# mLSTM's small f32 products in pairs of half arrays, and the prompt's negative maxima from one VectorE reduction

## The reference, cut to what matters

```python
qk = jnp.einsum('bthd,bshd->btsh', qc, kc) * w
num = jnp.einsum('btsh,bshe->bthe', qk, vc) + sc[..., None] * jnp.einsum('bhed,bthd->bthe', C, qc)
...
C_new = sl[..., None, None] * C + jnp.einsum('bsh,bshe,bshd->bhed', wl, vc, kc)
n_new = sl[..., None] * n + jnp.einsum('bsh,bshd->bhd', wl, kc)
```

## Time and profile before

| what | us |
|---|---|
| median of three runs (lowest, highest) | 1054.78 (1048.41, 1056.2) |
| the profiled execution: its time | 1056.03 |
| its span, first to last instruction | 1054.3 |
| TensorE busy | 1004.5 (95%) |
| VectorE busy | 615.4 (58%) |
| ScalarE busy, GpSimd busy | 403.9 (38%), 151.6 (14%) |
| mean granted TensorE clock, as a share of full speed | 0.985 |
| the mLSTM heads and what leads into the samples' attention | 285 to 372 |
| the prompt's attention, from the first maximum to the last value product | about 459 to 552 |

### The profile page before, as it was taken

One profiled execution on the slowest core, in us unless ns is written; L12 is line 12 of the kernel. 1 busy time (PEld: TensorE's weight loads), 2 busy tenths in 40 slices (PEclk: granted clock), 3 DMA queues, 4 the chain that ended last, 5 costly groups with the idle time before them and its releaser, 6 DMA issues.

```text
span 1054.3 us, 19143 instructions
## 1 busy us (share of the span) xinstructions
PE 1004.5 (95%) x7704; PEld 906.4 (86%) x7704; DVE 615.4 (58%) x1314; ACT 403.9 (38%) x759; POOL 151.6 (14%) x206
## 2 busy tenths in 40 slices
PE   4999999999999979989889999999999999999996
PEld 4999999899866647665559999999999999999996
DVE  3736753444358666677967556575757577832222
ACT  5223422333143455438764333333333334622222
POOL 3200020330112211016740000000000000000000
PEclk9999999999989999989999999999999999999998
DMA  6561162653611165344012222222222222423222
GB/s 188 194 179 41 44 200 72 244 185 145 244 37 52 53 255 210 117 121 136 1 55 103 82 82 84 83 83 82 82 82 82 82 82 57 119 68 87 77 55 90
DMA packets 82109, 114.29 MB, mean 108 GB/s; under 512 B 10075, under 2 KB 72681, under 8 KB 79296
## 3 DMA queue, kind: packets, MB, share of 16 engines
q1 hardware_dynamic: 75280, 70.60, 21.8%
q0 software_dynamic: 6768, 42.84, 11.0%
HBM read 103.33 MB, written 13.59 MB: 111 GB/s over the span
## 4 chain that ended last, share of the span: by engine, by line
PE 85%; DVE 8%; ACT 2%; issue 2%; DMA 1%; POOL 1%; SPq 0%; DVEq 0%; ACTq 0%
PE banks L1627 14%; PE banks L1625 12%; PE banks L1665 6%; PE banks L1128 6%; PE banks L1075 5%; PE banks L1664 5%; PE banks L1078 4%; PE banks L1079 4%; PE banks L1582 3%; PE banks L1112 3%; PE banks L1581 2%; PE banks L1696 2%; PE banks L1403 1%; PE banks L1339 1%; PE banks L1328 1%
## 5 line engine op out<-in xcount | busy, mean ns | idle before, releaser
L1627 PE MATMUL banks<-xnT_r,RB_r 128*128 128x320 f32 x352 | 109.6, 311 | 0.0
L1627 PE MATMUL banks<-xnT_r,ring_r 128*128 128x320 f32 x352 | 109.3, 311 | 0.0
L1625 PE MATMUL banks<-xnT_r,RB_r 128*128 128x256 f32 x352 | 103.1, 293 | 0.0
L1625 PE MATMUL banks<-xnT_r,ring_r 128*128 128x256 f32 x352 | 98.8, 281 | 0.0
L1627 PE MATMUL banks<-RC_r,RB_r 128*128 128x320 f32 x264 | 82.3, 312 | 0.0
L1625 PE MATMUL banks<-RC_r,RB_r 128*128 128x256 f32 x264 | 74.2, 281 | 0.0
L1128 PE MATMUL banks<-RA,RB 128*128 128x128 f32 (+1 forms) x512 | 71.0, 280 | 2.5 <-ACT RA L667 2.5
L2363 DVE TENSOR_TENSOR ring_r<-ring,RB_r 128x2048 fp32r<-128x2048 f32 x22 | 49.4, 2288 | 37.4 <-ACT RB_r L887 37.4
L1625 PEld LDWEIGHTS banks<-xnT_r,RB_r 128*128 128x128 f32 x352 | 67.0, 190 | 1.8
L1128 PEld LDWEIGHTS banks<-RA,RB 128*128 128x128 f32 x512 | 64.1, 188 | 4.0 <-ACT RA L667 3.9
L1625 PEld LDWEIGHTS banks<-xnT_r,ring_r 128*128 128x128 f32 x352 | 67.4, 192 | 0.0
(11 more groups left out here) (657 smaller groups left out, 2905.0 us busy)
## 6 DMA issues: line engine op xcount, KB each, us to landing
ring<-in_w_up_dram SPq DMA_DIRECT2D x22, 1024.0 KB
ring<-in_w_down_dram SPq DMA_DIRECT2D x8, 1408.0 KB, 6.8
ring<-in_w_in_dram SPq DMA_DIRECT2D x10, 1024.0 KB, 6.3
RB<-in_state_win_dram SPq DMA_DIRECT2D x8, 512.0 KB, 5.9
out_win_s_dram<-in_state_win_dram POOLq DMA_DIRECT2D x1, 4032.0 KB
xsp<-RC SPq DMA_DIRECT2D x1, 2304.0 KB, 7.7
xT<-xsp SPq DMA_DIRECT2D x1, 2304.0 KB, 15.0
RA<-in_x_prompt_dram SPq DMA_DIRECT2D x4, 512.0 KB, 5.3
```

The source lines that it names most:

```text
L1625: t.matmul(ps[4 + par][:, w * UA:(w + 1) * UA], wk[:, w, k, c], x[:, 0:UA], skip_group_check=True, **first)
L1627: last = t.matmul(ps[2 * par + w][:, 0:UB], wk[:, w, k, c], x[:, UA:T], **on)
```

## The change

1. `spread`: the three small products for the samples become one of 128 columns over `r12`, the stretch of `uT` in which `r1`'s last 64 and `r2`'s first 64 values lie side by side. `slc` is read out of its result with a stride.
2. The eight products with `C` alternate between output rows 0 to 63 and 64 to 127. VectorE adds the second half to the first when it copies to `hs`, with one operation more.
3. `kbd` is 128 rows by 4 sequences in place of 64 rows by 8: sequences 0 to 3 in the upper half, 4 to 7 in the lower. `vw` and the sample keys `mk` then stand in both halves, so `project` has one 64-row product more, VectorE one `vw` operation more, and the two products of L1290 take one half of the rows each.
4. The prompt's `n`: the four one-column products alternate between output row 0 and row 64; VectorE adds the two, one operation more.
5. The queries of the prompt and samples (`qT`) are written with `SCALE` in them, by a `scalar_tensor_tensor` in place of a `tensor_tensor` (sixteen of them), so that the exponentials of the prompt need no scale and the maxima no multiplication: `tensor_reduce` with `negate=True` writes the negative maxima, and L2268 is gone from all 32 units. `Qbd`, the samples' own queries, stays as it was.

```diff
-                t.matmul(ps[1][0:NSMP, 256:256 + NSMP], selh[:, h, 0:NSMP], r1[:, SEQ:T], start=True, stop=True)
-                t.matmul(ps[1][:, 256 + NSMP:256 + 2 * NSMP], selh[:, h, :], r2[:, 0:NSMP], start=True, stop=True)
-                t.matmul(ps[1][:, 256 + 2 * NSMP:256 + 2 * NSMP + NB], selh[:, h, :], r2[:, TS - 1:NSMP:TS], start=True,
-                         stop=True).then_inc(S("m_spread"), 1)
+                t.matmul(ps[1][:, 256:256 + 2 * NSMP], selh[:, h, :], r12, start=True, stop=True)\
+                    .then_inc(S("m_spread"), 1)
...
-                t.matmul(ps[1][0:NSMP, P:2 * P], ucT[:, h, SEQ:T], wqk[:, 1, h, :], start=True,
-                         stop=True).then_inc(S("m_proj"), 1)
+                for r in range(2):
+                    last = t.matmul(ps[1][NSMP * r:NSMP * (r + 1), P:2 * P], ucT[:, h, SEQ:T], wqk[:, 1, h, :], start=True, stop=True)
+                last.then_inc(S("m_proj"), 1)
...
-                out = ps[6][0:NSMP, P + 1:2 * (P + 1)]
+                out, odd = (ps[6][NSMP * r:NSMP * (r + 1), P + 1:2 * (P + 1)] for r in range(2))
...
-                    last = t.matmul(out, Qm[:, b, :], CT[:, b, :], start=False, stop=(b == NB - 1))
+                    last = t.matmul(out if b % 2 == 0 else odd, Qm[:, b, :], CT[:, b, :], start=(b == 1), stop=(b >= NB - 2))
...
-                    t.matmul(ps[2 * x][:, :], vw[0:NSMP, 4, :],
-                             kbd[0:NSMP, 4 * x:4 * x + 4, :].rearrange("p b d -> p (b d)"),
+                    half = slice(NSMP * x, NSMP * (x + 1))
+                    t.matmul(ps[2 * x][:, :], vw[half, 4, :], kbd[half, :, :].rearrange("p b d -> p (b d)"),
...
-                    t.matmul(ps[7][0:1, P:2 * P], rcol[:, 2, i, h:h + 1], mk[:, i, :], start=(i == 0), stop=(i == 3))
+                    at = NSMP * (i % 2)
+                    t.matmul(ps[7][at:at + 1, P:2 * P], rcol[:, 2, i, h:h + 1], mk[:, i, :], start=(i < 2), stop=(i >= 2))
...
-                        v.tensor_tensor(qT[to, g, 0:TA], bank[at, 0:TA], rstd_b[at, 0:TA], ALU.mult)
+                        v.scalar_tensor_tensor(out=qT[to, g, 0:TA], in0=bank[at, 0:TA], scalar=SCALE, in1=rstd_b[at, 0:TA],
+                                               op0=ALU.mult, op1=ALU.mult)
...
-                v.tensor_scalar(vw[0:NSMP, 4, :], mv[0:NSMP, 4, h, 0:P], rcol[0:NSMP, 2, 4, h:h + 1], None, ALU.mult)
+                for r in range(2):
+                    v.tensor_scalar(vw[NSMP * r:NSMP * (r + 1), 4, :], mv[0:NSMP, 4, h, 0:P], rcol[0:NSMP, 2, 4, h:h + 1], None,
+                                    ALU.mult)
...
-                v.scalar_tensor_tensor(out=kbd[0:NSMP, :, :], in0=bmask.unsqueeze(2).to_broadcast([NSMP, NB, P]), scalar=0.0,
-                                       in1=mk[0:NSMP, 4:5, :].to_broadcast([NSMP, NB, P]), op0=ALU.is_equal,
+                v.scalar_tensor_tensor(out=kbd, in0=bm2.unsqueeze(2).to_broadcast([P, NB // 2, P]), scalar=0.0,
+                                       in1=mk[:, 4:5, :].to_broadcast([P, NB // 2, P]), op0=ALU.is_equal,
...
+                link(v.tensor_copy(hs[0:NSMP, 4, h, :], ps[6][0:NSMP, P + 1:2 * (P + 1)]))
                 v.tensor_copy(hs[:, 0:3, h, :], ps[5][:, 0:3 * (P + 1)].rearrange("p (i e) -> p i e", i=3))
                 v.tensor_copy(hs[:, 3, h, :], ps[6][:, 0:P + 1])
-                v.tensor_copy(hs[0:NSMP, 4, h, :], ps[6][0:NSMP, P + 1:2 * (P + 1)]).then_inc(S("m_numd"), 1)
+                v.tensor_tensor(hs[0:NSMP, 4, h, :], ps[6][NSMP:P, P + 1:2 * (P + 1)], hs[0:NSMP, 4, h, :],
+                                ALU.add).then_inc(S("m_numd"), 1)
...
-                v.tensor_copy(npo[:, h * P:(h + 1) * P], ps[7][0:1, P:2 * P])
+                link(v.tensor_copy(npo[:, h * P:(h + 1) * P], ps[7][0:1, P:2 * P]))
+                v.tensor_tensor(npo[:, h * P:(h + 1) * P], ps[7][NSMP:NSMP + 1, P:2 * P], npo[:, h * P:(h + 1) * P], ALU.add)
...
-                link(v.tensor_reduce(cst[:, u % 4, 0, :], both[:, :, 0:(i + 1) * P], AX.X, ALU.max))
-                v.tensor_scalar(cst[:, u % 4, 1, :], cst[:, u % 4, 0, :], -SCALE, None, ALU.mult).then_inc(S("p_max"), 1)
+                v.tensor_reduce(cst[:, u % 4, 1, :], both[:, :, 0:(i + 1) * P], AX.X, ALU.max, negate=True).then_inc(S("p_max"), 1)
```

More of the change, by code:

```diff
@@ L177, in hybrid_decoder_layer @@
         b4 = carve(RB, [("E", EW + NSMP), ("W", EW + NSMP), ("mqT", T), ("mkT", T), ("mk", NTILE * P), ("Cst", NB * P),
-                        ("CT", NB * (P + 1)), ("kbd", NB * P), ("Qm", NB * NSMP)])
+                        ("CT", NB * (P + 1)), ("kbd", NB // 2 * P), ("bm2", NB // 2), ("Qm", NB * NSMP)])
         E, W, mqT, mkT = b4["E"], b4["W"], b4["mqT"], b4["mkT"]
@@ L183, in hybrid_decoder_layer @@
         CT = b4["CT"].rearrange("p (b e) -> p b e", b=NB)
-        kbd = b4["kbd"].rearrange("p (b d) -> p b d", b=NB)
+        kbd, bm2 = b4["kbd"].rearrange("p (b d) -> p b d", b=NB // 2), b4["bm2"]
         Qm = b4["Qm"].rearrange("p (b t) -> p b t", b=NB)
@@ L189, in hybrid_decoder_layer @@
         r0, r1, r2, r3 = (c["uT"][0:MH, n * T:(n + 1) * T] for n in range(4))
+        r12 = c["uT"][0:MH, T + SEQ:T + SEQ + 2 * NSMP]
         restart, down = RA[0:MH, 2 * CVW:2 * CVW + T], RA[0:MH, 2 * CVW + T:2 * (CVW + T)]
@@ L807, in _ @@
                     act.wait_ge(S("cmp_dve"), 1)
-                    a.activation(Pc, Pc, ACT.Exp, scale=SCALE).then_inc(S("s_ce"), 1)
+                    a.activation(Pc, Pc, ACT.Exp).then_inc(S("s_ce"), 1)
                 if p:
@@ L826, in exp_unit @@
                     last = a.activation(Pb[u % 4][:, h, 0:n], ps[2 * (u % 2) + h][:, 0:n], ACT.Exp,
-                                        bias=cst[:, u % 4, 1, h:h + 1], scale=SCALE, accum_out=cst[:, u % 4, 2, h:h + 1])
+                                        bias=cst[:, u % 4, 1, h:h + 1], accum_out=cst[:, u % 4, 2, h:h + 1])
                 last.then_inc(S("p_exp"), 1)
@@ L1880, in _ @@
                         g, at = 2 * (i % 2) + r, slice(HD * r, HD * r + HD)
-                        v.tensor_tensor(qT[to, g, 0:TA], bank[at, 0:TA], rstd_b[at, 0:TA], ALU.mult)
-                        v.tensor_tensor(qT[to, g, TA:T], smp[at, 0:TB], rstd_b[at, TA:T], ALU.mult)
+                        v.scalar_tensor_tensor(out=qT[to, g, 0:TA], in0=bank[at, 0:TA], scalar=SCALE, in1=rstd_b[at, 0:TA],
+                                               op0=ALU.mult, op1=ALU.mult)
+                        v.scalar_tensor_tensor(out=qT[to, g, TA:T], in0=smp[at, 0:TB], scalar=SCALE, in1=rstd_b[at, TA:T],
+                                               op0=ALU.mult, op1=ALU.mult)
                         last = v.tensor_tensor(Qbd[to, :, h * 32 + g * TS:h * 32 + g * TS + TS],
@@ L2033, in _ @@
             bmask = smask[0:NSMP, TS - 1:NSMP:TS]
+            for r in range(2):
+                v.tensor_copy(bm2[NSMP * r:NSMP * (r + 1), :], bmask[:, NB // 2 * r:NB // 2 * (r + 1)])
             sh = lambda x: x.rearrange("p (i h) -> p i h", i=NTILE)
@@ L2067, in _ @@
                 v.tensor_scalar(mkT[:, SEQ:T], ps[1][:, NSMP:2 * NSMP], KSCALE, None, ALU.mult)
-                link(v.tensor_scalar(mk[0:NSMP, 4, :], ps[1][0:NSMP, P:2 * P], KSCALE, None, ALU.mult))
+                link(v.tensor_scalar(mk[:, 4, :], ps[1][:, P:2 * P], KSCALE, None, ALU.mult))
                 qd = Qm[:, 0, 0:1]
@@ L2072, in _ @@
                                 ps[1][:, 256 + NSMP:256 + 2 * NSMP].rearrange("p (b t) -> p b t", b=NB), ALU.mult)
-                v.tensor_copy(slc, ps[1][:, 256 + 2 * NSMP:256 + 2 * NSMP + NB]).then_inc(S("m_projd"), 1)
+                v.tensor_copy(slc, ps[1][:, 256 + NSMP + TS - 1:256 + 2 * NSMP:TS]).then_inc(S("m_projd"), 1)
                 v.tensor_copy(CT[:, :, P], vcol[:, V_N + h:V_N + 32:MH])
```

## The result

| | median, us (lowest, highest; runs) |
|---|---|
| before, beside the change | 1055.08 (1048.41, 1059.21; 20) |
| after | 1048.28 (1045.26, 1054.95; 20) |
| ratio after / before, 95% interval | 0.9944 (0.9928 to 0.9961) |
| after, run once more on another chip | 1049.33, ratio 0.9951 (0.9929 to 0.9972) |

The change is some 0.5% faster: 6.8 us between the medians of the first comparison, 5.5 in the second. So its sign and its range held, and its gain is three to four us too large. Where these went is what the experiments are about. By the number alone the forecast can't be told from two of its rivals, which stood at 1048.4 (the maxima don't gain) and 1050 (the pairs don't run side by side); only the traces tell them apart. The profiled executions took 1056.03 before and 1047.63 after, 8.4 us apart.

The account below looks back on a forecast made before the run. TensorE and waits interrupting it were taken to bound the kernel. 6.4 us from mLSTM plus 3.2 from the maxima made 9.6 less: 1054.8 to 1045.2 us, with 1041 to 1050 as the forecast's own range.

Parts of the forecast that it names:

- the maxima don't gain: Rival for the prompt's attention: negation costs, or the waits just move, giving 1048.4 us; chance 0.10.
- the pairs don't run side by side: Rival for TensorE's paired small products: they might still be serial, giving 1050 us; chance 0.14.
- What bounds: Whole kernel: TensorE holds 85% of the chain of waits; in mLSTM heads TensorE would then wait 0.6 us for VectorE.
- The pairs: mLSTM's small TensorE products: L1286 1.92 to 1.03 us, L1290 1.91 to 1.06, L1296 0.96 to 0.51, spreads 0.79 to 0.27.
- The round: One mLSTM head at full clock: 17.12 us against 18.89, 1.77 less in heads 1 and 2, 1.29 in head 3.
- Head 0: First mLSTM head, which waits for ScalarE's exponentials first: 2.0 us less from spreads, project and L1286.
- The tail: VectorE's end of the mLSTM stage after head 3's last L1286: 0.4 us more, from two added sum operations.
- The maxima: Prompt's attention: dropping L2268 gives 3.2 us less, with VectorE mostly waiting for GpSimd one instruction later, at L2275.
- The queries: Sixteen query evacuations of 0.455 us become at worst 0.1 longer each, covered by TensorE's work; counted as nothing.
- the prompt gains the waiting too: Rival for the prompt's attention: early maxima let engines close up, some 8 us from that stage, 1040.4 us; chance 0.20.
- The clock rival: Rival, slower: low clock stays in mLSTM heads 1 to 3; two whole heads give 1076 us; chance 0.04.
- The prediction's own sign of being wrong: Wrong if paired products keep 1.9 us, the reduction grows, or the granted clock in 310 to 370 is no longer full.

Follow-up runs that it names:

- changed_again: The changed kernel timed once more, unaltered, on another chip: 1049.33 us, 0.9951 of the kernel before.
- prompt_only: The kernel before with only the negated maxima and the scale in the queries, mLSTM as before: 0.9969 of the kernel before.
- prompt_again: The kernel before with only the prompt's part of the change, timed a second time: 1051.04 us, 0.9959 of the kernel before.
- mlstm_only: The kernel before with only the mLSTM parts of the change, maxima and queries as before: 0.999 of the kernel before.
- spare_scale: The changed kernel with the multiplication back on VectorE, on an unread tile behind each maxima reduction's signal: 0.9973 of the kernel before.
- tail_wait: The kernel before with only the prompt's part, plus eight repeated VectorE reciprocals lengthening TensorE's wait for the last head: 1054.48 us.
- buffers_split: The changed kernel with a second buffer for C's first half and project's wait for VectorE split in two: 0.9891 of the kernel before.

## Why the prediction was right, and where it was not

1. **What bounds.** Right: TensorE and the waits that interrupt it. With TensorE's products shorter, VectorE is what it waits for.
2. **The pairs.** Right in every term on TensorE. L1286 takes 1.05 in the chain (1.03 forecast), the update's products 1.13 in the timeline (the 1.06 of the chain plus the overlap), the one-column products 0.54 to the next start (0.51), the spread 0.22 in the chain of `changed_again` (0.27). The added product in `project` costs nothing (0.10): 331.53 - 327.91 = 3.62 as before. So one-column weights, 129 columns and two halves of one bank all run in pairs.
3. **The round.** The step that failed. The prediction made it of TensorE and VectorE, and its piece "L1251 to L1244: 1.37" took what was the case before. It measured 333.61 - 331.53 = 2.08, because the buffer of `C` comes back too late. Every other piece of the round stands: 3.65 for 3.58, 3.62 for 3.72, 4.61 for 4.63, 3.92 for 3.82 (value products and `C`). The gain of heads 1 to 3 at full clock is then 2.5 us (56.18 us before, from L1286 to L1286, and three times 17.88 after) where 4.8 were forecast; the store and reload are 1.9 of the missing 2.3, rounds of 17.24 in place of 17.12 the rest. The path was hidden before by little. In the trace of before the same load for head 2 was issued at 332.39 and had landed at 335.43, 0.3 us ahead of the L1244 that reads it (timeline, then chain):

```profile
332.39 1.43 SPq L2610 DMA_DIRECT2D RB<-in_state_mlstm_C_dram  x2
```

```profile
335.74 0.59 PE banks L1244 x4
```

A margin of 0.3 us, spent by the first 0.3 of a gain of 1.77. The Trainium skill (DMA: Bandwidth & Descriptors, Anatomy of one DMA) gives a DMA that GpSimd issues a fixed cost of about 2 us beside its bytes, so an estimate by it is 2.6 us for the store of 256 KB, and for the load too if SyncE's queue is no different; the chain has 2.80 and 2.98, so the estimate is 0.2 to 0.4 low, and would still have shown two such transfers in a row as a term of over 5 us.

Head 0, forecast at 2.0, gained 1.4: from the first spread to the last L1286 it took 20.4 us with the old mLSTM part (`prompt_only`, `prompt_again`) and 19.0 with the new one (the kernel after, `mlstm_only`, `spare_scale`), each with equally much half clock in it. No run says which of its terms was too large.

4. **The tail.** Its length was right: from the end of the last L1286 to L1251 6.53 us before (370.88 - 364.35), 6.95 after (368.47 - 361.52), 0.42 more for 0.4. What followed was missed: the wait that it is for TensorE, 2.40 us, and the half clock behind.
5. **The maxima.** Right in size, 3.3 us for 3.2. The waits pass to the factor's product as forecast, but only half of them (4.6 of some 9 us), so VectorE's busy time there fell by 10.4 us where 6 or a little more were expected. The reciprocal between them keeps its 155 ns. The reduction does not grow.
6. **The queries.** Right: their evacuation has a median of 456 ns, 455 before.
7. **The rivals.** That the prompt gains the waiting too, that pairs stay serial and that maxima don't gain all fell. The clock rival named the mechanism, waits of TensorE with less work about them, but put it in heads 1 to 3. The prediction's own sign of being wrong did come up there: the kernel after has a granted clock of 0.57 at 356 to 360, and its L1281 at 355.96 takes 4.14 us in place of 2.50. But such stretches stand in heads 1 to 3 of three of four profiles with the old mLSTM part (`prompt_only`, `prompt_again`, `tail_wait`) and six of ten with the new one, so the change did not bring them. The one that it brought lies behind the stage, and costs 1.5 to 3 us and not 20. The Trainium skill (TensorE: Matmul & The Clock Gate, Why this matters for your kernels) warns only of longer gaps than this one; the traces disagree, with half clock behind waits of 1.55 to 2.47 us in eight profiles.

Added up: 3.4 us from mLSTM at the same half clock and 3.3 from the prompt make 6.7, in place of 6.4 and 3.2. The half clock behind the stage takes 1.5 to 3 back, which leaves 3.7 to 5.2. Measured are 5.5 and 6.8. The rest is not settled: executions of one kernel lie 10 us apart, by their low-clock stretches. The forecast's range held partly by its width of 9 us, since mLSTM gave little more than half of what was forecast for it.

## What to carry to other kernels

When a loop gets shorter, write down every path that closes once per round, the stores and reloads of a reused buffer too, with what each has in hand now: the smallest margin is what the gain can be before that path needs an edit of its own. Cutting TensorE's work where another engine sets the end only lengthens its wait, and here the wait itself cost clock afterwards; look at the granted clock behind each wait that grows. Of the two pairings that were undone, the one ahead of the signal that VectorE waits for paid 0.55 us a round, and the one behind it cost 0.2 to 0.4, since its copies were work for VectorE. The pairs of the one-column products and the merged spread were not tested alone.

## What the runs showed of the hardware

- A TensorE wait of 1.55 to 2.47 us between busy stretches was followed, 0.5 to 2.0 us after its end, by 7 to 17 us at 1.2 GHz in eight of nine profiles. With 1.65 us of throw-away transposes inside it, both profiled kernels stayed at 2.4 GHz; one of the two, `buffers_split`, had stayed there without them too.
- A store of 256 KB and the load that waits for it took 5.99 to 6.28 us from the last write of VectorE to the first read of TensorE, in three heads of each of seven profiles.
- A small VectorE operation behind a reduction is as dear as GpSimd makes it: 468 ns in the mean before, 537 in `spare_scale`, with 168 and 157 as the shortest; taking it away handed half of the wait to the next one with two SBUF inputs, and not to the reciprocal.
